# The eight-column time-step products spread over the projection unit that follows them

## Chip, cores and metric

The kernel runs on one core of one Trainium2 chip. The metric is the device time of one execution in microseconds (us); the kernel before has a median of 1232.65 us over 3 runs (1232.53 to 1235.9).

## The reference

Two transformer-like blocks follow each other on 256 tokens of width 1024, all in float32. The first block projects the normalised, modulated input `h` with one wide matrix and splits the result by columns; three mixers use the parts. The change concerns one part of eight columns, the raw time steps of the state-space mixer:

```python
h = rms_norm(x, g_pre_mix) * (1 + scale1) + shift1
(sc_b, sc_c, sc_x, q, k, v, z, xbc, dt_raw,
 gl_a, gl_b, gl_c) = split_columns(h @ w_in)
...
dt = jax.nn.softplus(dt_raw.astype(jnp.float32) + dt_bias.astype(jnp.float32))
a_neg = -jnp.exp(a_log.astype(jnp.float32))
y = ssd_scan(xh, dt, a_neg, bm, cm) + xh * d_skip.astype(jnp.float32)[:, None]
```

`dt_raw` is 256 tokens by 8 heads, a product over 1024 inputs. The second block ends in a feed-forward layer in which each token reads 128 experts from HBM.

## The kernel before, in words

Everything is written out by engine: each engine (PE for the matrix products, DVE, ACT and POOL for the rest, SP for most transfers) has its own program, and semaphores tie them together. Tokens are two tiles of 128 (`NT`), the width is eight chunks of 128 (`KC`). The weights come as units of 128 x 2048 float32 (1 MB) through a ring of three slots; the order of the units is the list `ORDER` (three "xbc", three "sc", two "qk", one "v", two "z", twelve "gl", and so on), and SP loads a slot again when `unit_done` says that PE is through with its former unit.

The projection units up to ("sc", 0) are plain float32 products of `hT` (the transposed input) with the unit. From ("sc", 1) on (`FRONT0`), `proj_T` (line 559) makes the first half of the sum over the width in plain float32 (line 568: eight products, of which each stands as two records in the trace), and the second half from two rounded parts (`mm3`, lines 527 to 529: three products each, eight times, one record each). The rounded parts of a unit are written by ACT (`front_hi`, line 1259) and POOL (`front_lo`, line 1592); PE waits for them between the two halves (`front_parts`). ACT copies each finished unit out of its PSUM bank (line 1246).

Between the units ("sc", 0) and ("sc", 1) stand the time-step products (lines 661 to 665): for each of the 2 token tiles and 8 chunks, a 128 x 128 piece of `hT` is the stationary operand and 8 columns of `w_dt` are the moving one, 16 products, or 32 records. They accumulate in the PSUM bank `BX`, after a wait for its former reader (`evac` at 3). The last increments `dt_mm`.

DVE waits for `dt_mm` (line 1890) behind its 24 convolution steps (lines 1876 and 1879), makes three short steps that end in `dt_lin`, then sums the modulation units 8 and 9 (lines 1798 and 1801), and then waits for ACT's exponential (line 1305), which ACT makes only after it has copied ("sc", 2) out and split the unit after next. SP's loads of the modulation units 10 and 11 (line 433) wait for DVE's sums of 8 and 9 and stand in SP's program behind the load of ring unit 7 and before that of ring unit 8, the "v" unit.

Further on, PE has another batch of narrow products (line 926: 16 products with one column, 32 records) ahead of the products that are made in a pause (line 831). Lines 748 and 749 alternate 256-column and 128-column products; lines 689, 708, 709, 690 and 711 mix products over 64 partitions with such over 128.

Of the kernel before, what the change touches and what calls it, by code (L numbers as in the profile page):

```python
# [25 lines left out]
P = 128  # L26
D = 1024
T = 256
NT = T // P
KC = D // P  # L30
# [88 lines left out]
def build(nc, stream, mod_w, small, x, band, final_g, experts, out):  # L119
    with ExitStack() as ctx:  # L120
        start = {}
# [5 lines left out]
        def sem(name):  # L127
            return ctx.enter_context(nc.semaphore(name))
# [6 lines left out]
        def cut(t, at, *dims):  # L135

            n = int(np.prod(dims))
            v = t[:, at:at + n]
            if len(dims) == 2:
                return v.rearrange("p (a b) -> p a b", a=dims[0])  # L140
            if len(dims) == 3:
                return v.rearrange("p (a b c) -> p a b c", a=dims[0], b=dims[1])
            return v
# [12 lines left out]
        hT = hT_flat[:, :].rearrange("p (k t) -> p k t", k=KC)  # L156
# [12 lines left out]
        ps = ctx.enter_context(nc.psum_tensor("ps", [P, 8, 512], F32))  # L169
        BM, BX = 2, 7  # L170
# [20 lines left out]
        def c_(name, a=0, b=None):  # L191
            lo, hi = SMALL[name]
            return sm[:, lo + a:(hi if b is None else lo + b)]
# [47 lines left out]
        def query_arrived(h):  # L241
# [7 lines left out]
        sc = cut(areaA, 3090, 6, T)  # L249
# [83 lines left out]
        dt_mm, dt_lin, dt_exp, dt_one, dt_log, a_exp, a_ready = (  # L333
            sem("dt_mm"), sem("dt_lin"), sem("dt_exp"), sem("dt_one"), sem("dt_log"), sem("a_exp"), sem("a_ready"))
# [136 lines left out]
        def _(pe):  # L471
            mm = nc.tensor.matmul

            def arrived(kind, j):
                u = AT[kind, j]
                if kind == "wq":
                    pe.wait_ge(*query_arrived(j))
                    return query_w[j]
                if (kind, j) == ("wo2", 2):
                    pe.wait_ge(wo2_in, 16)  # L480
                    return spare[:, :]
                pe.wait_ge(w_in[u % RING], 16 * (u // RING + 1))
                return slot[u % RING]
# [23 lines left out]
            def gemm_T(w, bank, rhs, new=None):  # L507

                for b in range(2):
                    for k in range(KC):  # L510
                        if new is not None and b == 0:
                            hT_chunk(new, k)
                        at = (b * KC + k) * P
                        last = mm(ps[:, bank, b * T:(b + 1) * T], w[:, at:at + P], rhs[:, k, :],  # L514
                                  start=(k == 0), stop=(k == KC - 1))
                return last
# [8 lines left out]
            def mm3(o, lhs, rhs, start, stop, **kw):  # L525

                mm(o, lhs[1], rhs[0], start=start, stop=False, **kw)  # L527
                mm(o, lhs[0], rhs[1], start=False, stop=False, **kw)  # L528
                return mm(o, lhs[0], rhs[0], start=False, stop=stop, **kw)  # L529
# [14 lines left out]
            def bank_free():  # L544

                n = evacs[0]
                evacs[0] += 1
                if n >= 2:
                    pe.wait_ge(evac, n - 1)
                return n % 2  # L550

            def front_parts(u):

                if u == FRONT0:
                    pe.wait_ge(hq_lo_ready, 1)
                pe.wait_ge(front_lo_ready, u - FRONT0 + 1)
                return front_hi[u % 2], front_lo[u % 2]

            def proj_T(kind, j):

                u, w, bank = AT[kind, j], arrived(kind, j), bank_free()
                if u < FRONT0:
                    gemm_T(w, bank, hT).then_inc(unit_done, 1)
                    return
                for b in range(2):
                    for k in range(4):
                        at = (b * KC + k) * P
                        mm(ps[:, bank, b * T:(b + 1) * T], w[:, at:at + P], hT[:, k, :], start=(b == 0 and k == 0),  # L568
                           stop=False, skip_group_check=True)
                both = front_parts(u)  # L570
                for b in range(2):
                    for k in range(4):
                        last = mm3(ps[:, bank, b * T:(b + 1) * T], [v[:, b, k * P:(k + 1) * P] for v in both],
                                   [v[:, k, :] for v in (hq_h, hq_l)], False, k == 3, skip_group_check=True)
                last.then_inc(unit_done, 1)

            def transposes(n):
# [79 lines left out]
            xbc_part(2, 2, 3, 4, 5, 6, 7)  # L657
            evacs[0] = 3
            proj_T("sc", 0)
            pe.wait_ge(evac, 3)  # L660
            for t in range(NT):
                for k in range(KC):
                    last = mm(ps[:, BX, 8 * t:8 * t + 8], hT[:, k, t * P:(t + 1) * P],
                              c_("w_dt", 8 * k, 8 * k + 8), start=(k == 0), stop=(k == KC - 1))
            last.then_inc(dt_mm, 1)
            for j in range(1, 3):
                proj_T("sc", j)
            for j in range(2):
                proj_T("qk", j)
            w = arrived("v", 0)  # L670
            bank = bank_free()
            for t in range(NT):
                for k in range(4):
                    mm(ps[:, bank, t * T:(t + 1) * T], hT[:, k, t * P:(t + 1) * P], w[:, k * T:(k + 1) * T],
                       start=(t == 0 and k == 0), stop=False, skip_group_check=True)
            both = front_parts(AT["v", 0])
            for t in range(NT):
                for k in range(4):
                    last = mm3(ps[:, bank, t * T:(t + 1) * T], [v[:, k, t * P:(t + 1) * P] for v in (hq_h, hq_l)],
                               [v[:, k // 2, (k % 2) * T:(k % 2 + 1) * T] for v in both], False, k == 3,  # L680
                               skip_group_check=True)
            last.then_inc(unit_done, 1)

            def sb_scores(h, part, stop):

                r = slice(64 * (h % 2), 64 * (h % 2) + 64)
                q, k = qk[r, h // 2, :], qk[r, 2 + h // 2, :]
                if part == 0:
                    return mm(ps[:, B3 + h, 0:T], k[:, 0:P], q[:, :], start=True, stop=stop)
                return mm(ps[:, B3 + h, T:T + P], k[:, P:T], q[:, P:T], start=True, stop=stop)  # L690

            pe.wait_ge(evac, 8)
            for h in range(4):
                sb_scores(h, 0, True)
                last = sb_scores(h, 1, True)
# [3 lines left out]
            for j in range(12):  # L699
# [3 lines left out]
                if j == 2:  # L703
                    pe.wait_ge(sb_lk, 1)
                    for h in range(4):
# [5 lines left out]
                        last = mm(ps[:, B3 + h, T:T + P], c_("suffix"), sbl[:, h, T:T + P], start=False, stop=True)  # L711
                    last.then_inc(sb_sum, 1)
                if j in (3, 4):

                    t = j - 3
# [3 lines left out]
                    for b in range(4):  # L719
                        last = nc.tensor.transpose(ps[:, BX, b * P:(b + 1) * P], xbc[:, b, t * P:(t + 1) * P],  # L720
                                                   c_("ident"))
# [9 lines left out]
                if j == 6:  # L731
# [3 lines left out]
                    for h in range(4):  # L735
# [3 lines left out]
                        last = mm(o[:, P:T], v1[:, 1, 64 * h:64 * h + 64], sba[:, h, T:T + P], start=False, stop=True,  # L739
                                  skip_group_check=True)  # L740
# [4 lines left out]
                    for h in range(8):  # L745
# [3 lines left out]
                        last = mm(o[:, P:T], a_rep[:, 8 + h, :], c_("tri"), start=False, stop=True,  # L749
                                  skip_group_check=True)  # L750
                    last.then_inc(acs_mm, 1)
                if j == 7:

                    pe.wait_ge(dec_arg, 16)
                    for g in range(2):
                        r = slice(64 * g, 64 * g + 64)
                        mm(ps[:, B3 + g, 0:T], xbc[r, 4, 0:P], xbc[r, 5, :], start=True, stop=True)
                        last = mm(ps[:, B3 + g, T:T + P], xbc[r, 4, P:T], xbc[r, 5, P:T], start=True, stop=True)
                    last.then_inc(bc_mm, 1)
                if j == 8:  # L760

                    pe.wait_ge(w_ready, 16)
                    for h in range(8):
                        r = slice(64 * (h % 2), 64 * (h % 2) + 64)
                        b = h // 2
                        o = ps[r, B3 + 2 + b // 2, (b % 2) * T:(b % 2) * T + T]
                        mm(o, x_tok[:, 0, 64 * h:64 * h + 64], decay[:, h, 0:T], start=True, stop=True)
                        last = mm(o[:, P:T], x_tok[:, 1, 64 * h:64 * h + 64], decay[:, h, T:T + P], start=False, stop=True,
                                  skip_group_check=True)
                    last.then_inc(y_mm, 1)  # L770
                if j == 9:
# [3 lines left out]
                    for g in range(2):  # L775
                        for b in range(2):
                            last = mm(ps[:, BX, g * T:(g + 1) * T], c_("ones"), ysq[:, 2 * g + b, :], start=(b == 0),
                                      stop=(b == 1))
# [3 lines left out]
            for j in range(4):  # L782
# [8 lines left out]
                for n, y in enumerate((ya, yb)):  # L791
                    for b in range(2):
                        for k in range(2):
                            mm(ps[:, banks[n], b * T:(b + 1) * T], w[:, at:at + P], y[:, k, :],
                               start=(k == 0), stop=(k == 1))
# [3 lines left out]
                for b in range(2):  # L799
                    for k in range(4):  # L800
                        at = (4 * b + k) * P
                        last = mm3(ps[:, banks[2], b * T:(b + 1) * T], [v[:, at:at + P] for v in both],
                                   [v[:, k, :] for v in (yc_h, yc_l)], k == 0, k == 3)
# [7 lines left out]
            for t in range(NT):  # L811
                for j in range(2, 4):
                    last = wo_tile(j, t)
# [109 lines left out]
            for b in range(2):  # L923
                for k in range(KC):
                    at = (b * KC + k) * P
                    last = mm(ps[:, BX, b:b + 1], w[:, at:at + P], modT[:, 72 + k:73 + k], start=(k == 0),
                              stop=(k == KC - 1))
# [81 lines left out]
            for g in range(4):  # L1009
                o = ps[:, g // 2, (g % 2) * T:(g % 2) * T + T]  # L1010
                mm(o, u2[:, 0, g * P:(g + 1) * P], band_sb[:, 0, g, :], start=True, stop=True)
                last = mm(o[:, P:T], u2[:, 1, g * P:(g + 1) * P], band_sb[:, 1, g, P:T], start=False, stop=True,
                          skip_group_check=True)
# [11 lines left out]
            for g in range(4):  # L1025
                last = mm(ps[:, g // 2, (g % 2) * T:(g % 2) * T + T], c_("pool_w", g * P, (g + 1) * P),
                          pooled[:, g, :], start=True, stop=True)
# [1567 lines left out]
```

## Time and profile before

| | |
|---|---|
| median of 3 runs | 1232.65 us (1232.53, 1232.65, 1235.9) |
| the profiled execution's own time | 1235.79 us |
| its span in the trace | 1234.1 us |
| mean granted TensorE clock | 0.971 |
| PE busy / DVE busy / ACT busy / POOL busy | 90% / 71% / 40% / 38% |
| mean read rate of the memory | 334 GB/s |

The span runs from the first to the last instruction of the trace; the execution's own time is 1.7 us longer. The profiled execution is 3.1 us slower than the median of the runs. The granted clock is given as a share of full speed: 1.00 is 2.4 GHz, 0.50 is 1.2 GHz.

### The profile page before, as it was taken

The numbers are of one execution on the slowest core, as the hardware profiler recorded it, in microseconds if no ns is written. First come the engines' busy times: TensorE is split into PE (matmuls) and PEld (weight loads), VectorE is DVE, ScalarE is ACT, GpSimd is POOL, SyncE is SP. The second block draws the span as 40 slices with busy tenths as digits, with TensorE's granted clock in tenths as the row PEclk, the third lists the DMA queues.
The fourth block names the chain that finished last, engine by engine and source line by source line (L and its number), as shares of the span: only waits on it lengthen the run. The fifth ranks groups of instructions, "written<-read, shape, count | busy, mean of one in ns | idle before, by whom it ended". The sixth has DMA issues, their size and how long they took to land.

```text
span 1234.1 us, 14550 instructions
## 1 busy us (share of the span) xinstructions
PE 1105.7 (90%) x4858; PEld 738.4 (60%) x4858; DVE 879.7 (71%) x1944; ACT 495.1 (40%) x1134; POOL 468.3 (38%) x360
## 2 busy tenths in 40 slices
PE   3999999999999999999899999987777878778776
PEld 3899899969999998875555655423323333223222
DVE  6586468987888888837787957758668586685555
ACT  2225153263333335534544344433434334325334
POOL 0133333023554452303355445743533535444420
PEclk9999999999999999999999999999998988989998
DMA  9656775664767773664999999999999999999995
GB/s 382 260 208 235 283 265 198 239 240 171 314 281 281 314 320 157 228 249 166 419 392 422 421 422 421 421 422 421 421 422 421 422 421 422 421 420 422 420 422 204
DMA packets 57803, 413.07 MB, mean 335 GB/s; under 512 B 6544, under 2 KB 6544, under 8 KB 8208
## 3 DMA queue, kind: packets, MB, share of 16 engines
q0 software_dynamic: 41328, 296.24, 58.3%
q1 hardware_dynamic: 16272, 115.83, 23.8%
q8 instruction: 30, 0.49, 0.2%
q10 hardware_dynamic: 144, 0.26, 0.1%
q14 instruction: 29, 0.24, 0.1%
HBM read 411.26 MB, written 1.05 MB: 334 GB/s over the span
## 4 chain that ended last, share of the span: by engine, by line
PE 59%; DMA 30%; DVE 6%; ACT 3%; issue 1%; POOL 1%; SPq 0%; ACTq 0%; DVEq 0%; POOLq 0%
PE ps L1111 14%; PE ps L527 8%; PE ps L529 7%; PE ps L528 7%; DMA areas_seam<-in_experts,idx 6%; DMA spare<-in_experts,idx 6%; PE ps L568 5%; PE ps L514 4%; DMA areaB<-in_experts,idx 4%; DMA gate_area<-in_experts,idx 3%; DMA mod_ring<-in_experts,idx 3%; DMA ring<-in_experts,idx 3%; DMA ring<-in_experts,part_buf 2%; PE ps L640 2%; DMA areaB<-in_mod_w 2%; PE ps L494 1%
## 5 line engine op out<-in xcount | busy, mean ns | idle before, releaser
L1515 ACT ACTIVATE act<-now 128x1 f32<-128x1 f32 x256 | 50.8, 198 | 264.4 <-DVE now L2389 261.7
L1111 PE MATMUL ps<-areaB,mod_sum 128*128 128x512 f32 x232 | 114.0, 623 | 25.4 <-ACT mod_sum L1523 25.4
L1801 DVE SCALAR_TENSOR_TENSOR mod_sum<-mod_ring,cols,mod_sum 128x256 f32<-128x256 f32 x280 | 118.9, 499 | 0.0
L1612 POOL TENSOR_TENSOR w_lo<-ring,w_hi 128x512 fp32r<-128x512 f32 x41 | 97.8, 2402 | 45.1 <-ACT w_hi L1253 44.9
L1669 POOL DMA_INDIRECT areaB<-in_experts,idx x58 | 68.3, 1178 | 118.6 <-PE ps L1111 58.5
L1111 PE MATMUL ps<-ring,mod_sum 128*128 128x512 f32 x192 | 95.7, 630 | 15.8 <-ACT mod_sum L1523 15.1
L1523 ACT ACTIVATE mod_sum<-small,act 128x128 f32<-128x128 f32 x256 | 102.8, 402 | 16.1 <-ACT act L1519 0.4
L1253 ACT ACTIVATE w_hi<-ring 128x2048 fp32r<-128x2048 f32 x41 | 78.5, 1914 | 53.3 <-DMA ring<-in_stream 43.2
L527 PE MATMUL ps<-hT_h,w_lo 128*128 128x256 f32 x352 | 98.4, 279 | 0.8 <-DVE hid_l L2069 0.8
L2389 DVE CUSTOM_DVE_ANT_0 areaB<-areaB,xn 128x1024 f32<-128x1024 f32 x58 | 70.8, 1225 | 38.7 <-DMA areaB<-in_experts,idx 38.6
L529 PE MATMUL ps<-hT_h,w_hi 128*128 128x256 f32 x352 | 98.2, 279 | 0.0
L528 PE MATMUL ps<-hT_l,w_hi 128*128 128x256 f32 x352 | 98.1, 279 | 0.0
L1812 DVE TENSOR_TENSOR w_lo<-ring,w_hi 128x1536 fp32r<-128x1536 f32 x41 | 89.1, 2196 | 11.4 <-ACT w_hi L1253 11.3
L1111 PEld LDWEIGHTS ps<-areaB,mod_sum 128*128 128x128 f32 x232 | 43.4, 195 | 89.6 <-ACT mod_sum L1523 45.3
L1592 POOL TENSOR_TENSOR front_lo<-ring,front_hi 128x1024 fp32r<-128x1024 f32 x19 | 57.8, 3044 | 88.7 <-ACT front_hi L1259 88.7
L1111 PE MATMUL ps<-gate_area,mod_sum 128*128 128x512 f32 x156 | 77.9, 623 | 13.5 <-ACT mod_sum L1523 13.4
L2389 DVE CUSTOM_DVE_ANT_0 ring<-ring,xn 128x1024 f32<-128x1024 f32 x48 | 58.3, 1224 | 31.8 <-DMA ring<-in_experts,idx 31.6
L1519 ACT ACTIVATE act<-act,gate_buf 128x1 f32<-128x1 f32 x256 | 75.4, 295 | 9.3
L1111 PEld LDWEIGHTS ps<-ring,mod_sum 128*128 128x128 f32 x192 | 36.7, 200 | 69.5 <-issue 37.0
L1669 POOL DMA_INDIRECT ring<-in_experts,idx x47 | 51.7, 1101 | 70.1 <-PE ps L1111 53.0
L2389 DVE CUSTOM_DVE_ANT_0 gate_area<-gate_area,xn 128x1024 f32<-128x1024 f32 x39 | 47.8, 1226 | 32.2 <-DMA gate_area<-in_experts,idx 32.1
L1111 PE MATMUL ps<-mod_ring,mod_sum 128*128 128x512 f32 x120 | 59.3, 618 | 9.3 <-ACT mod_sum L1523 8.8
(446 smaller groups left out, 2611.3 us busy)
## 6 DMA issues: line engine op xcount, KB each, us to landing
ring<-in_stream SPq DMA_DIRECT2D x75, 1024.0 KB, 6.0
mod_ring<-in_mod_w POOLq DMA_DIRECT2D x24, 1024.0 KB, 6.1
mod_ring<-in_mod_w SPq DMA_DIRECT2D x18, 1024.0 KB, 5.9
gate_area<-in_mod_w SPq DMA_DIRECT2D x3, 1024.0 KB, 13.2
areaB<-in_mod_w SPq DMA_DIRECT2D x3, 1024.0 KB, 22.9
gate_area<-in_stream SPq DMA_DIRECT2D x3, 1024.0 KB, 13.1
small<-in_small SPq DMA_DIRECT2D x1, 1352.0 KB, 28.7
x_sb<-in_x SPq DMA_DIRECT2D x1, 1024.0 KB, 9.0
```

Of the source, the lines that this page charges most:

```text
L527: mm(o, lhs[1], rhs[0], start=start, stop=False, **kw)
L528: mm(o, lhs[0], rhs[1], start=False, stop=False, **kw)
L529: return mm(o, lhs[0], rhs[0], start=False, stop=stop, **kw)
L1111: last = mm(ps[:, B3 + 2 * b + t, :], spread_w[n // FEW % 2][:, n % FEW, :], row[ROW_OF[n]][:, D + 512 * b:D + 512 * b + 512], start=first ...
L1253: A(w_hi[u % RING], slot[u % RING], ACT.Identity).then_inc(hi_ready, 1)
L1519: step(A(weight, weight, ACT.Identity, scale=gate_h[h % 2][:, t, n % TOPK:n % TOPK + 1]))
L1523: A(spread_w[n // FEW % 2][:, n % FEW, :], c_("ident"), ACT.Identity, scale=weight)\
L1612: nc.gpsimd.tensor_tensor(w_lo[s][:, HALF:], slot[s][:, HALF:], w_hi[s][:, HALF:].bitcast(F32), ALU.subtract).then_inc(lo_pool, 1)
L1669: pool.indirect_dma_start(row[ROW_OF[n]], None, experts, bass.IndirectOffsetOnAxis(ap=idx[:, n:n + 1], axis=0))\
L1801: ins = V.scalar_tensor_tensor(out=o[n], in0=w, scalar=vec[:, k:k + 1], in1=o[n], op0=ALU.mult, op1=ALU.add)
L1812: V.tensor_tensor(w_lo[s][:, 0:HALF], slot[s][:, 0:HALF], w_hi[s][:, 0:HALF].bitcast(F32), ALU.subtract).then_inc(lo_dve, 1)
L2389: V.tensor_tensor_reduce(u, u, xn[:, t, :], 1.0, 0.0, ALU.mult, ALU.add, now[n // FEW % 4][:, n % FEW:n % FEW + 1]).then_inc(dot_done, 1)
```

## The change

`proj_T` gets an argument, a function that it calls after each of the eight plain products (with 0 and the product's number) and after each of the eight threefold products (with 1 and the number). The time-step products of the first token tile are made in the first half of unit ("sc", 1), one after each of its plain products, those of the second tile in the second half. Only the very first of the sixteen now has `start` set. The wait for bank `BX` stays where it was; `dt_mm` is incremented by the last of them, which is PE's last product before unit ("sc", 2).

```diff
-            def proj_T(kind, j):
+            def proj_T(kind, j, between=None):
 
                 u, w, bank = AT[kind, j], arrived(kind, j), bank_free()
...
                         mm(ps[:, bank, b * T:(b + 1) * T], w[:, at:at + P], hT[:, k, :], start=(b == 0 and k == 0),
                            stop=False, skip_group_check=True)
+                        if between:
+                            between(0, 4 * b + k)
                 both = front_parts(u)
                 for b in range(2):
                     for k in range(4):
                         last = mm3(ps[:, bank, b * T:(b + 1) * T], [v[:, b, k * P:(k + 1) * P] for v in both],
                                    [v[:, k, :] for v in (hq_h, hq_l)], False, k == 3, skip_group_check=True)
+                        if between:
+                            between(1, 4 * b + k)
                 last.then_inc(unit_done, 1)
...
             proj_T("sc", 0)
             pe.wait_ge(evac, 3)
-            for t in range(NT):
-                for k in range(KC):
-                    last = mm(ps[:, BX, 8 * t:8 * t + 8], hT[:, k, t * P:(t + 1) * P],
-                              c_("w_dt", 8 * k, 8 * k + 8), start=(k == 0), stop=(k == KC - 1))
-            last.then_inc(dt_mm, 1)
-            for j in range(1, 3):
-                proj_T("sc", j)
+
+            def dt_product(t, k):
+
+                last = mm(ps[:, BX, 8 * t:8 * t + 8], hT[:, k, t * P:(t + 1) * P], c_("w_dt", 8 * k, 8 * k + 8),
+                          start=(t == 0 and k == 0), stop=(k == KC - 1), skip_group_check=True)
+                if t == NT - 1 and k == KC - 1:
+                    last.then_inc(dt_mm, 1)
+
+            proj_T("sc", 1, dt_product)
+            proj_T("sc", 2)
```

## Rows read from the trace of the kernel before

**Rows 1.** The page: span, granted clock in 40 slices, chain by engine.

```profile
span 1234.1 us, 14550 instructions
...
PEclk9999999999999999999999999999998988989998
...
PE 59%; DMA 30%; DVE 6%; ACT 3%; issue 1%; POOL 1%; SPq 0%; ACTq 0%; DVEq 0%; POOLq 0%
```

**Rows 2.** The chain that ended last, 50 to 80 us: start, us, what.

```profile
52.82 6.91 PE ps L514 x32
59.73 3.47 PE ps L663 x32
63.20 5.24 PE ps L568 x16
...
71.31 3.45 PE ps L568 x16
...
77.63 2.37 PE ps L568 x11
```

**Rows 3.** Single microseconds of the same stretch: busy times by engine, granted clock.

```profile
62.00:63.00 1.00, 1.00 (x11) 1.00 (x10) 1.00 (x1) 0.00 (x0) 1.00 (x1) 1.00 1.04 442
...
64.00:65.00 1.00, 1.00 (x4) 0.82 (x3) 1.00 (x3) 0.00 (x0) 0.07 (x1) 0.50 0.06 16
...
67.00:68.00 1.00, 1.00 (x6) 0.90 (x5) 0.97 (x6) 0.00 (x0) 0.00 (x0) 1.00 0.00 0
```

**Rows 4.** The chain, 460 to 640 us, and the clock of one microsecond in it.

```profile
473.16 3.46 PE ps L926 x32
476.63 3.52 PE ps L831 x8
...
481.02 0.86 PE ps L831 x4
...
478.00:479.00 1.00, 1.00 (x4) 0.82 (x3) 0.84 (x4) 1.00 (x4) 0.00 (x0) 0.50 0.00 0
```

**Rows 5.** Weight loads of the time-step products (name, count, shortest, median, longest in ns).

```profile
L663 PEld LDWEIGHTS ps<-small,hT x32: 190/192/192, 59.4 to 62.9; 128*128 128x128 f32 x32
```

**Rows 6.** Timeline of PE: wide and narrow float32 products in turn (lines 748, 749).

```profile
171.78 0.60 PE L748 MATMUL ps<-small,areaB 128*128 128x256 f32 x2
172.22 0.38 PE L749 MATMUL ps<-small,areaB 128*128 128x128 f32 x2
172.44 0.60 PE L748 MATMUL ps<-small,areaB 128*128 128x256 f32 x2
```

**Rows 7.** PE where 64 and 128 partitions alternate: one head, then the granted clock.

```profile
131.71 0.70 PE L689 MATMUL ps<-areaA 64*128 64x256 f32 x2
...
134.02 0.70 PE L689 MATMUL ps<-areaA 64*128 64x256 f32 x2
...
131.80:141.03 9.23, 9.23 (x41) 1.00 0.68 273
```

**Rows 8.** Timeline of DVE around the time steps.

```profile
54.02 13.62 DVE L1879 SCALAR_TENSOR_TENSOR areaA<-areaA,small 128x256 f32<-128x256 f32 x18
67.56 0.16 DVE L1891 TENSOR_TENSOR dtb<-ps,small 128x16 f32<-128x16 f32 x1
...
68.46 5.63 DVE L1801 SCALAR_TENSOR_TENSOR mod_sum<-mod_ring,cols,mod_sum 128x256 f32<-128x256 f32 x14
79.34 2.33 DVE L1900 TENSOR_SCALAR dtb<-dtb 128x16 f32<-128x16 f32 x1 [5.26 <-ACT dtb L1305]
```

**Rows 9.** Timeline of POOL: the rounded parts of units ("sc", 1) and ("sc", 2).

```profile
57.08 2.53 POOL L1592 TENSOR_TENSOR front_lo<-ring,front_hi 128x1024 fp32r<-128x1024 f32 x1
61.39 2.69 POOL L1592 TENSOR_TENSOR front_lo<-ring,front_hi 128x1024 fp32r<-128x1024 f32 x1 [1.78 <-ACT front_hi L1259]
```

**Rows 10.** SP's loads of modulation units 10, 11; ACT's split of ring unit 8.

```profile
73.72 0.80 SPq L433 DMA_DIRECT2D mod_ring<-in_mod_w  x2
...
85.32 1.06 ACT L1259 ACTIVATE front_hi<-ring 128x1024 fp32r<-128x1024 f32 x1 [0.74 <-DMA ring<-in_stream]
```

## The prediction

> **What bounds the kernel now.** The page comes first: the chain that ended last is PE for 59% of its length and transfers for 30%, and the clock row shows almost full speed in the stretch of the change [rows 1]. So a step that leaves PE shorter near the start should carry through, unless another engine or a transfer is close behind. The chain in order of time shows that here nothing but PE stands on it [rows 2]: unit ("sc", 0) from 52.82, the 32 time-step records from 59.73, the plain half of ("sc", 1) from 63.20, and so on without a gap. Two things are to be read there. The 32 records take 3.47 us, 108 ns each, although each moves only eight columns. And the plain half of ("sc", 1), 16 records, takes 5.24 us, where the same half of ("sc", 2) takes 3.45 us.
>
> The reason for the second is in the microseconds of that stretch [rows 3]: the clock is 1.00 (2.4 GHz) during the narrow records and 0.50 (1.2 GHz) after them, and back at 1.00 at 67. PE had been busy the whole time before it fell, with nothing but narrow products in its last 3.5 us. The price of the low clock is 5.24 - 3.45 = 1.79 us. The same picture comes once more: 32 one-column records from 473.16 to 476.63, then the clock at 0.50, and eight records of line 831 in 3.52 us, where four of them at the full clock take 0.86, so eight 1.72 [rows 4]. Price: 1.80 us. Both batches are followed by a fall in this execution; nothing shows that they are in every one.
>
> **The change, part by part.**
>
> *The 16 products themselves.* None is removed, none added. Their rate is set by the stationary load: each takes 192 ns as recorded [rows 5], and one starts every 108 ns. Placed after a wide product, a narrow one still needs its load, and the next wide one needs its own, which can only be hidden under the narrow one. The nearest row for that is the alternation of 256 and 128 columns [rows 6]: four records in 172.44 - 171.78 = 0.66 us; two wide ones at 3.45 / 16 = 0.216 us [rows 2] leave 0.23 for two narrow ones, so 0.11 each. A narrow record between wide ones costs what it costs in a batch. 32 x 0.108 = 3.47 before; 32 x 0.115 = 3.7 at most by this row. The lower bound is a narrow record that hides altogether: 0 instead of 3.47 us, which no row shows. I take the alternating row, as it is the nearest: a change of 0 to +0.2 us, and 0.1 in the sum.
>
> The Trainium skill ("TensorE: Matmul & The Clock Gate", in the section on why the gap is 56 ns and not 53.3 ns) says that the start-to-start distance of products never falls below some 25 ns however few columns there are, and its opening table says that weight loads are pulled ahead of products in flight. By these two, 32 well hidden records would cost an estimated 0.8 us. The 0.66 us of rows 6 speak against it.
>
> *The change of kind.* In the second half the narrow float32 products stand between products of rounded operands: 8 insertions, 16 changes of kind. Each unit now has two such changes. ("sc", 2) lasts from 71.31 to 77.63, 6.32 us [rows 2]: 3.45 for the plain half, 2.87 for 24 records, 0.120 each, and nothing left for a change. I take 0. The upper bound is from a stretch where products over 64 and over 128 partitions alternate: one head, ten records (four wide, six narrow), takes 134.02 - 131.71 = 2.31 us [rows 7], against 4 x 0.216 + 6 x 0.11 = 1.52, so 0.8 us for four changes, 0.2 each. Over 16 changes that is 3.2 us, over all 32 places 6.4. That row changes the partitions, which this change does not.
>
> *The clock.* After the change no stretch holds narrow products alone: in the first half two records of 0.216 us stand to two of 0.11, in the second three of 0.12 to two. The stretch of rows 7, over 9 us of wide and narrow mixed with gaps between, has 1.00 throughout. So the fall at 63 us should be gone: -1.79 us in an execution that had it, and 0 in one that had not.
>
> *The start of ("sc", 1).* It moves forward by 3.47 us, to 59.73. Its rounded part is written by 57.08 + 2.53 = 59.61 [rows 9], and it is asked for only after the plain half with its eight insertions, at about 59.73 + 3.45 + 1.8 = 65.0. That of ("sc", 2) is done at 64.1, needed after 73. No new wait for PE.
>
> *The later `dt_mm`.* It moves from 63.20 to 59.73 + 3.45 + 2.87 + 3.5 = 69.6. DVE is ready for it at 67.56 [rows 8], so it waits some 2 us where it waited for nothing. Behind that wait are the three short steps and the sums of units 8 and 9, which then end near 76.1 in place of 74.1. Next DVE waits for ACT's exponential, 5.26 us long now; that comes 1.8 us earlier if the clock does not fall, so about 1.5 us of wait are left. Price 0; if the cover were gone, 2 us of DVE, not of PE. ACT gets `dt_lin` at 70 and asks for it after 75.
>
> *SP's queue.* The loads of units 10 and 11 follow DVE's sum and go out at about 75.7 in place of 73.72 [rows 10], in front of the load of ring unit 8, due when ("sc", 2) is over, at 69.5 + 6.3 = 75.8. Three megabytes then land at about 85, when unit 8 landed before too (ACT waited 0.74 us for it, to 85.32). ACT's split ends at 86.4, POOL's part at 2.7 [rows 9] more is there at 89.1, and PE asks for it two units and a plain half after the start of ("qk", 0), 77.63 + 2 x 6.32 + 3.45 = 93.7 before, 91.9 now. It is nearly 3 us from being a wait. Price 0.
>
> **The sum** against the profiled execution: 1.79 - 0.1 = 1.7 us less, span 1232.4, own time 1234.1. Against the median another reading is needed. The profiled execution is 1235.79, one of the three runs is 1235.9, the other two are 1232.53 and 1232.65, and the distance of 3.1 to 3.4 us is near the sum of the two falls, 1.79 + 1.80 = 3.6. The likeliest reading is that the clock falls behind both batches in some executions and behind neither in others, and that the median is one of the others. Then there is nothing to win in it: 1232.65 + 0.1, rounded 1232.7.
>
> **The rivals.** A difference of 0.3% (3.7 us) is about what a measurement of this kernel can tell from no change.
>
> (A) The forecast, nothing in the median: 1232.7 us, chance 0.46.
>
> (B) The fall at 63 us is in the median execution too, and the 3.3 us between the runs have another cause. For it: the profiled execution has it. Then 1232.65 - 1.7 = 1230.9 us. If the shift also takes the batch at 473 us out of its fall, 1229.1. Chance 0.30, the last part of it 0.04.
>
> (C) The narrow products hide under the wide ones. Against it: rows 6. 1232.65 - 3.47 = 1229.2, and 1227.4 with the clock. Chance 0.05.
>
> (D) The other side: each change between narrow and wide costs as in rows 7, on PE, on the path. 16 x 0.2 = 3.2 gives 1235.9, 32 x 0.2 = 6.4 gives 1239.1 (1237.3 if a fall goes). It decides from 3.7 / 32 = 0.12 us for each place on. Against it: the 6.32 us of a unit with two changes. Chance 0.07.
>
> (E) The median execution of the new kernel is one in which the clock falls behind the second batch alone, while the old median had neither: 1232.7 + 1.8 = 1234.5. Chance 0.12.
>
> That the change does not do what it says is hardly open: the batch either stands in the trace as one piece or does not.
>
> **How the numbers follow.** 1232.7 is the time of (A). From 1229.8 to 1235.2 the range takes in (A), (B) without its last part, and (E), and leaves out (C), most of (D) and the double gain, 0.16 or so with some noise. Faster by over 0.3%, below 1228.95, needs (C) with the clock or more than (B) gives: 0.05. Slower, above 1236.35, needs (D) at its upper bound: 0.05. The same: 0.90.
>
> **What would show it.** In the new profile: line 568 of ("sc", 1) and the inserted records in turn from about 59.7, the unit over at 69.5 (9.8 us for both); granted clock 1.00 from 60 to 70; DVE idle for 2 us before its step at 67.56; its wait for ACT shorter; no wait of PE before ("sc", 1)'s second half or in "v". (C) would show as a unit well under 9 us, (D) as one of 13 us or more. The forecast is wrong if the runs of the new kernel are below 1231.5 with the clock low in the old one's runs, which makes it (B), or above 1235.

## The result, and the profile after

In 21 runs of each kernel the changed kernel takes 1237.73 us (1235.07 to 1241.54) and the kernel before 1235.9 us (1232.49 to 1238.99). The ratio is 1.0021, with a 95% interval of 1.0013 to 1.0028. The change costs 2.6 us by the ratio. That is within the 0.3% named as what a measurement can tell, but outside the forecast range of 1229.8 to 1235.2 us, and it is slower where no change was forecast. The kernel before, too, has a higher median than the three runs that were known: 14 of its 21 runs take 1235.1 us or more, 7 take 1233.8 or less, and two of the three were among the 7. The profiled execution has a span of 1237.0 us against 1234.1.

| us | before | after |
|---|---|---|
| unit ("sc", 0), line 514, starts | 52.82 | 53.12 |
| unit ("sc", 2), line 568, starts | 71.31 | 69.83 |
| SP loads modulation units 10, 11 | 73.72 | 78.13 |
| the "v" unit has landed (ACT's split starts) | 85.32 | 89.24 |
| 16 records of line 494 behind the first "gu" units | 294.44 | 297.46 |
| span | 1234.1 | 1237.0 |

The starts of PE in the table and in the sums are those of the chain. The timeline puts the start of a group some 0.15 us earlier (69.67 for the 69.83 here).

The timeline of PE in the changed kernel shows the unit with the inserted products [rows 2]:

```profile
60.44 0.68 PE L568 MATMUL ps<-hT,ring 128*128 128x256 f32 x2
60.95 0.28 PE L668 MATMUL ps<-small,hT 128*128 128x8 f32 x2
61.09 0.68 PE L568 MATMUL ps<-hT,ring 128*128 128x256 f32 x2
...
65.47 0.29 PE L668 MATMUL ps<-small,hT 128*128 128x8 f32 x2
...
66.05 0.28 PE L668 MATMUL ps<-small,hT 128*128 128x8 f32 x2
...
69.67 3.70 PE L568 MATMUL ps<-hT,ring 128*128 128x256 f32 x16
...
94.99 0.39 PE L527 MATMUL ps<-front_hi,hq_l 128*128 128x256 f32 x1 [2.01 <-POOL front_lo L1599]
```

A plain product with its insertion comes every 0.65 us, a threefold one with its insertion every 0.58 us, so the narrow pair costs 0.22 in both, and a change of kind costs nothing. PE is 1.5 us ahead at ("sc", 2), although it started 0.3 us later. The last line is new: PE waits 2 us for POOL in the "v" unit. Ahead of the same unit's plain half it already waits for the unit itself:

```profile
89.26 3.72 PE L681 MATMUL ps<-ring,hT 128*128 128x256 f32 x16 [0.38 <-DMA ring<-in_stream]
```

From the start of ("sc", 2) to the second half of "v" PE takes 25.3 us (69.67 to 94.99), where it took 22.2 before (71.15 to 93.38). Of these 3.1 us the two waits show 2.4. The rest does not appear as idle time, as the ends of the records ahead of a wait are modelled. What leads to both waits stands on the other engines. First DVE, then one of its steps by itself, then SP [rows 8, 10]:

```profile
69.85 0.17 DVE L1898 TENSOR_TENSOR dtb<-ps,small 128x16 f32<-128x16 f32 x1 [1.90 <-PE ps L668]
...
70.75 7.75 DVE L1808 SCALAR_TENSOR_TENSOR mod_sum<-mod_ring,cols,mod_sum 128x256 f32<-128x256 f32 x14
```

```profile
71.54 2.60 DVE L1808 SCALAR_TENSOR_TENSOR mod_sum<-mod_ring,cols,mod_sum 128x256 f32<-128x256 f32 x1
```

```profile
78.13 0.80 SPq L433 DMA_DIRECT2D mod_ring<-in_mod_w  x2
78.97 0.43 SPq L423 DMA_DIRECT2D ring<-in_stream  x1
```

The chain of work from 80 us on takes up the thread. In the kernel before nothing but PE stood on it here:

```profile
78.97 10.24 DMA ring<-in_stream
89.24 1.07 ACT front_hi L1266
90.38 4.58 POOL front_lo L1599
94.99 0.39 PE ps L527
```

DVE waits 1.90 us for the last narrow product. Its 14 steps of sums then take 7.75 us, where they took 5.63 in [rows 8]: one of them takes 2.60 us where the shortest takes 0.47, and it starts at 71.54, while POOL's split of a weight unit runs (71.35 to 73.85). SP's two modulation loads wait for these sums, and the load of the "v" unit stands behind them. It goes out at 78.97, 2.7 us after ("sc", 2) is over and it could have gone. Three megabytes asked for within 1.3 us take till 89.24 (a fourth is asked for at 82.59), and ACT, POOL and PE follow one by one.

The clock is at 1.00 where it had fallen to 0.50 [rows 3], and at 0.50 where it had been at 1.00. From the single microseconds of the changed kernel (the granted clock is the third number from the end of a line):

```profile
64.00:65.00 1.00, 1.00 (x8) 0.91 (x7) 1.00 (x3) 0.00 (x0) 0.38 (x1) 1.00 0.22 82
...
280.00:281.00 1.00, 1.00 (x6) 1.00 (x6) 0.90 (x3) 0.98 (x2) 1.00 (x3) 0.50 0.95 401
```

The table closes with this: 0.3 us from the start of the execution, -1.8 us to the start of ("sc", 2), +3.0 us up to the products behind "v" (line 689 starts at 96.59 before, and its successor, line 696, at 98.12), +1.5 us between 260 and 294 us. The sum is 3.0, and the spans differ by 2.9.

### The profile page after: what moved, and what is told of

It reads as the page before. It is cut to its first block, busy times and chain, and to the rows that moved or that the text cites. A ratio compares the mean times of both kernels' runs of the same rounds, so it can differ in the third digit from the quotient of the medians.

```text
span 1237.0 us, 14550 instructions
## 1 busy us (share of the span) xinstructions
PE 1101.6 (89%) x4858; PEld 736.3 (60%) x4858; DVE 877.0 (71%) x1944; ACT 495.3 (40%) x1134; POOL 468.5 (38%) x360
## 4 chain that ended last, share of the span: by engine, by line
PE 55%; DMA 30%; DVE 8%; ACT 4%; POOL 1%; issue 1%; SPq 0%; ACTq 0%; DVEq 0%; POOLq 0%
PE ps L1118 14%; PE ps L527 7%; PE ps L528 7%; PE ps L529 7%; DMA areas_seam<-in_experts,idx 6%; DMA spare<-in_experts,idx 6%; PE ps L514 4%; PE ps L568 4%; DMA areaB<-in_experts,idx 3%; DMA mod_ring<-in_experts,idx 3%; DMA gate_area<-in_experts,idx 3%; DMA ring<-in_experts,idx 3%; DMA ring<-in_experts,part_buf 2%; PE ps L644 2%; DMA areaB<-in_mod_w 2%; PE ps L494 1%
## 5 line engine op out<-in xcount | busy, mean ns | idle before, releaser
L1260 ACT ACTIVATE w_hi<-ring 128x2048 fp32r<-128x2048 f32 x41 | 78.5, 1914 | 53.1 <-DMA ring<-in_stream 43.1
L1819 DVE TENSOR_TENSOR w_lo<-ring,w_hi 128x1536 fp32r<-128x1536 f32 x41 | 89.1, 2196 | 11.4 <-ACT w_hi L1260 11.3
```

The source lines that it names most:

```text
L1260: A(w_hi[u % RING], slot[u % RING], ACT.Identity).then_inc(hi_ready, 1)
L1819: V.tensor_tensor(w_lo[s][:, 0:HALF], slot[s][:, 0:HALF], w_hi[s][:, 0:HALF].bitcast(F32), ALU.subtract).then_inc(lo_dve, 1)
```

## The experiments

My theory after the result had two parts: the loss is a wait handed on from DVE over SP's queue to PE, and what the spread products gain in clock is given back in a fall near 275 us (279 in the changed kernel). The rival was that the inserted products themselves cost PE more than the batch. All ratios are to the kernel before, run on the same chip.

**1. DVE's sums ahead of its wait** (changed kernel).

```diff
+            mod_units(8, 10)
             dve.wait_ge(dt_mm, 1)
...
             V.tensor_scalar(lin, lin, 0.0, None, ALU.max).then_inc(dt_lin, 1)
-            mod_units(8, 10)
```

> The changed kernel, with DVE's sums of modulation units 8 and 9 moved ahead of its wait for the time-step products. Theory Q (the loss is a wait handed on: DVE's later sums hold back SP's loads of units 10 and 11, these hold back the load of the v unit, and PE waits for its rounded part): the sums end near 74 us, SP issues the loads of 10 and 11 by 74.5, the load of the v unit goes out at 76.3, PE has no wait in the v unit, and the time is 2.4 us below the changed kernel's, level with the kernel before or up to 1.8 us under it (ratio 0.9985 to 1.000). Rival R (the inserted products cost PE more than the batch, wherever they make other work wait): the unit ends where it does now and the time stays 1.5 us or more above the kernel before (ratio 1.0012 or more).

Measured: 0.9999 (0.9986 to 1.0011). PE has no wait in "v"; SP issues the two loads at 70.83. (The times of this profile, and of most that follow, lie up to 3 us ahead of those of the changed kernel from the start on, for a reason that experiment 7 shows.) The stall is gone with the products still spread over both halves.

**2. SP's loads of 10 and 11 behind the "v" unit** (changed kernel).

```diff
-MODS_BEHIND_LOAD = {2: 8, AT["sc", 1] + RING: 10, AT["qk", 1] + RING: 12, AT["z", 1] + RING: 14,
+MODS_BEHIND_LOAD = {2: 8, AT["sc", 2] + RING: 10, AT["qk", 1] + RING: 12, AT["z", 1] + RING: 14,
```

> The changed kernel, with SP's loads of modulation units 10 and 11 put behind the load of the v unit in place of ahead of it. Theory Q: the v unit lands by 83 us, ACT splits it right after its copy of the first qk unit, PE has no wait in v, DVE still waits 1.9 us for the time steps and its sums still end near 78.5, and the time is about 2.4 us below the changed kernel's (ratio to the kernel before 0.9985 to 1.000). Rival R: as slow as the changed kernel, ratio 1.002. A third (the two loads come too late for DVE's next sums, and that is passed on): DVE waits for them at 86 us and the gain is 1 us or less.

Measured: 0.9997 (0.9987 to 1.0007), no wait of PE in "v". DVE waits as long for PE (1.89 us) and its sums take as long (7.75) as in the changed kernel; the whole profile lies 2.7 us earlier. This makes it the cleanest of the four: the late sums do no harm once the load of the weights does not queue behind them.

```profile
67.16 0.17 DVE L1898 TENSOR_TENSOR dtb<-ps,small 128x16 f32<-128x16 f32 x1 [1.89 <-PE ps L668]
...
68.06 7.75 DVE L1808 SCALAR_TENSOR_TENSOR mod_sum<-mod_ring,cols,mod_sum 128x256 f32<-128x256 f32 x14
```

**3. All sixteen in the first half** (changed kernel).

```diff
                         if between:
                             between(0, 4 * b + k)
+                            between(1, 4 * b + k)
...
-                        if between:
-                            between(1, 4 * b + k)
```

> The changed kernel, with all sixteen products in the first half of the unit, two after each plain product, none in the second half. The last of them is then over at 60.0 + 3.45 + 3.6 = 67.1 us, before DVE asks for them at 67.9. Theory Q: DVE does not wait, the sums end at 74 to 75, no wait of PE in v, ratio 0.9985 to 1.000. Rival R: ratio 1.002. The clock stays at 1.00 between 60 and 70 us by my reading, since two wide records stand to four narrow ones; if it falls there, 1.8 us come back.

Measured: 0.9995 (0.9985 to 1.0005). DVE does not wait, the sums take 5.63 us, PE does not wait, the clock stays at 1.00 in this unit.

**4. The late wait alone** (kernel before, batch in place).

```diff
             dve.wait_ge(dt_mm, 1)
+            dve.wait_ge(unit_done, DONE("sc", 1))
```

> The kernel before, its products in one batch as they were, but DVE waits for the end of unit (sc, 1) before it reads the time steps. Theory Q: this alone brings the loss: DVE waits 2 us (3.7 where the clock has fallen behind the batch), the v unit lands 3 to 5 us later, PE waits 2 to 4 us in v, and the time is 2 to 3 us above the kernel before (ratio 1.0015 to 1.0025). Rival R: nothing happens, ratio 1.000, as no product was spread.

Measured: 1.0040 (1.0026 to 1.0055). From the list of waits, 50 to 110 us:

```profile
DVE dtb L1892 <- PE ps L529: 3.8, 1, 3.8
...
PE ps L527 <- POOL front_lo L1592: 2.0, 1, 2.0
```

The same chain without a single product moved, so the rival is out. It is worse than the changed kernel and worse than expected. The batch and the fall behind it are as in the kernel before, so nothing is gained ahead of the wait, which is 3.77 us for DVE; and in its profile the clock falls at 98 and at 282 us as well. PE lies 3.4 us behind the first profile of the kernel before at the second half of "v" (96.80 against 93.38), 4.9 us at the first product of line 873 (278.82 against 273.94), and 6.4 us at the records of line 494 (300.68 against 294.27): the two further falls come with 1.5 us each.

**5. The batch, with the sums first** (kernel before; the edit of experiment 1).

> The kernel before with its batch, only DVE's sums of units 8 and 9 moved ahead of its wait for the time steps, as in the first experiment. Against that experiment it tells the spread apart from the batch with the wait out of the way. If the fall of the clock behind the batch were in every execution, this one would be 1.7 us slower than the spread products with the same DVE order (ratio to the kernel before 1.000 against 0.9986). If the fall only comes in some executions, or comes back in another place, the two are level within 0.6 us.

Measured: 1.0000 (0.9988 to 1.0013), level with the spread products in the same order. The two intervals reach 1.5 us either way, so the times alone do not rule out the 1.7 us named in the expectation; the profile is clearer. The fall behind the batch is there in it (0.50 at 63 us), and the one near 275 is not.

**6. First half and loads behind, together.**

> The candidate: all sixteen products in the first half of the unit, and SP's loads of units 10 and 11 behind the load of the v unit. Both repairs cure the same wait, so together they should give no more than one: ratio 0.999 to 1.000, PE without a wait in v. If it is below 0.9985, something else than the wait and the clock is in play.

Measured: 1.0003 (0.9990 to 1.0016), no wait of PE in "v". The second repair adds nothing that the runs show.

**7. The kernel before once more**, one execution with its profile.

> The kernel before, unchanged, for a second profile. Two readings of the first profile are open: the clock falls behind the batch at 63 us in every execution, or only in some. If the first granted rise of the clock comes some 2 us earlier here than at 36.3 us, as it did in the profiles of the first three experiments, the time is near 1232.6 and I expect no fall behind the batch; if it comes at 36, I expect the fall and 1235.8.

Measured: 1232.84 us, span 1231.1. The time came as expected, the missing fall did not: the clock rises early, at 30.1 us, and falls behind the batch all the same.

```profile
30.00:31.00 1.00, 0.79 (x5) 0.38 (x3) 1.00 (x3) 0.00 (x0) 0.00 (x0) 0.95 0.91 385
...
61.00:62.00 1.00, 1.00 (x4) 0.81 (x3) 1.00 (x2) 0.00 (x0) 0.54 (x1) 0.50 0.34 131
```

The chain in order of time has the same 3.47 and 5.24 us as [rows 2], 2.5 us sooner:

```profile
50.29 6.91 PE ps L514 x32
57.19 3.47 PE ps L663 x32
60.66 5.24 PE ps L568 x16
```

In the first profile the clock rose at 36.3 us. Thus 2.5 of the 3 us between these two executions are there at 57 us, from when the clock rises first and not from whether it falls later. That all executions of the two groups differ by this is likely, but only these two of this kernel have a profile.

**8. The batch made twice** (kernel before).

```diff
-            for t in range(NT):
+            for t in [0, 1, 0, 1]:
```

> The kernel before with the sixteen products made twice in a row (the second time over the first). The batch takes 6.94 us in place of 3.47. If only the products cost, the time rises by 3.47 us (ratio 1.0028). If a fall of the clock is now made certain where it was not before, it rises by 3.47 + 1.8 = 5.3 us against the executions without a fall (ratio 1.0035 to 1.0043), and the profile shows 0.50 within the batch or behind it. DVE should not wait, or for under 0.2 us (the batch ends at 66.7).

Measured: 1.0050 (1.0035 to 1.0065), some 6 us. The clock is at 0.50 from 64.3 to 74.5 us. The 64 narrow records take 9.61 us in the chain, not 6.94: once the clock has fallen within them, they are slower too, an estimated 0.21 us each in place of 0.108 (38 of them fit before 64.3, which leaves 26 for the last 5.5 us). DVE, which was not to wait, waits 1.73 us.

**9. PE's later work put back in its old place** (experiment 3 and four products that nothing reads).

```diff
             proj_T("sc", 1, dt_product)
+            for _ in range(4):
+                mm(ps[:, BM, T:2 * T], c_("ident"), hT[:, 0, :], start=True, stop=True)
             proj_T("sc", 2)
```

> The kernel with all sixteen products in the first half of the unit, and behind that unit four more wide products whose result nothing reads (eight records, 1.72 us). They put the rest of PE's work back to where it lies in the kernel before. What is asked: in the spread kernels so far the clock fell at 273 to 279 us, in the stretch where PE waits for the second normalised input, and in the batch kernels without a late wait it did not. If that depends on where in time the stretch lies, the fall at 273 to 279 is gone here and none at 63 takes its place: the four products cost 1.72 and give 1.4 back, ratio 1.0000 to 1.0008 to the kernel before. If the stretch now falls in any case, the time is 1.7 us above the first-half kernel (ratio 1.001 to 1.0015) and the profile shows 0.50 near 275.

Measured: 1.0004 (0.9992 to 1.0017). PE does 1.72 us more work than in experiment 3 and the time is the same within the intervals. The profile has no fall at 63 and none near 275, which is the first of the two outcomes set out above; the ratios alone (0.9995 and 1.0004, chips apart) would not tell the two apart.

**10. The two pauses filled** (experiment 3 and four products that nothing reads, at lines 873 and 881 of the kernel before).

```diff
+                def fill():
+                    for _ in range(2 if new == 1 else 0):
+                        mm(ps[:, BM, T:2 * T], c_("ident"), c_("keys", 0, T), start=True, stop=True)
...
                 def step(j, n):
...
+                    if (j, n) in ((0, 0), (0, 1)):
+                        fill()
                     if n:
```

> The kernel with all sixteen products in the first half, and four wide products whose result nothing reads in PE's two pauses of 0.95 and 0.83 us ahead of the products of line 873 and 881 (two in each, 0.86 us), so at no cost if they fit. If the fall at 273 to 279 comes from the little work in that stretch, it goes, and the time is 1.4 us below the first-half kernel: ratio 0.9985 to 0.9992 to the kernel before, the first version under it. If the fall stays, the ratio is 0.9995 to 1.0003, as it was.

Measured: 0.9988 (0.9977 to 0.9998). The stretch near 275 is now at the full clock. The same microsecond, first in experiment 3:

```profile
274.00:275.00 1.00, 1.00 (x7) 1.00 (x6) 1.00 (x3) 1.00 (x1) 1.00 (x2) 0.50 0.58 229
```

and here:

```profile
274.00:275.00 1.00, 1.00 (x11) 1.00 (x10) 1.00 (x3) 1.00 (x1) 1.00 (x3) 1.00 0.75 279
```

In this profile, however, the gain does not last. At the first one-column record PE is 1.4 us ahead of experiment 3 (469.27 against 470.70); the clock then falls within that batch, at 471.8, and stays low till 478.7, where it was low from 474.4 to 477.8 in experiment 3; and at 479 PE is 0.2 us behind (the next records of line 831 of the kernel before start at 478.93 against 478.72). So the better ratio rests on the eleven times, not on the profile.

**11. The same four products in the kernel before**, as a control.

> The control for the last one: the kernel before with its batch, and the same four wide products in the pauses. There was no fall in that stretch to take away, so the ratio should be 1.0000, or up to 1.0003 if the products do not quite fit; the fall behind the batch at 61 to 64 us stays.

Measured: 0.9998 (0.9987 to 1.0008), the fall behind the batch still there. By the time the filler costs nothing that shows, and it is of no use while the batch stands.

**12. The second batch mixed as well** (experiment 10 and the one-column products of line 926 with wide ones between them).

```diff
                     last = mm(ps[:, BX, b:b + 1], w[:, at:at + P], modT[:, 72 + k:73 + k], start=(k == 0),
-                              stop=(k == KC - 1))
+                              stop=(k == KC - 1), skip_group_check=True)
+                    if k % 4 == 2:
+                        products_in_pause(1)
             last.then_inc(shift_mm, 1)
-            products_in_pause(4)
```

> The last version (products in the first half, four wide products in the two pauses near 271 us), and at the second batch of narrow products, the one-column ones at 473 us, the four wide products of the pause that follows are made between them, one after every fourth, in place of behind them. No product is added. If a stretch of nothing but narrow products is what the clock falls behind, the fall at 472 to 479 us goes too, and up to 0.8 us more is saved, no more because DVE's normalised tile, not PE, is what the transposes then wait for: ratio 0.9980 to 0.9988 to the kernel before. If it stays, the ratio is that of the last version, 0.9988.

Measured: 0.9987 (0.9974 to 0.9999), about 1.6 us under the kernel before. The falls behind both batches [rows 2 to 4] and the one near 275 are gone. From the timeline of PE:

```profile
476.39 0.68 PE L837 MATMUL ps<-small 128*128 128x256 f32 x2
476.90 0.28 PE L938 MATMUL ps<-modT,mod_ring 128*128 128x1 f32 x2
478.42 1.09 PE L829 MATMUL ps<-small,xn 128*128 128x128 f32 x8 [1.24 <-DVE xn L1765]
```

As expected, PE then waits (1.24 us) for DVE. The ratios of experiments 10 and 12 do not tell the two apart. Its profile has a span of 1231.8 us; the first one of the kernel before, in which the clock also first rises late (36.3 us there, 37.0 here), has 1234.1. Experiments 10 and 12 are the versions that beat both kernels. Their intervals reach 0.9998 and 0.9999, so the gain is small and just clear of none, and they are the best two of eleven ratios.

## Why the prediction was wrong

*The products themselves*: right. "0 to +0.2 us" for their cost, from the alternating row, against 0.22 us a pair in both halves. *The change of kind*: right at 0; rival (D) is out by experiments 1 to 3. Rival (C) is out for loads of this kind, and with it the estimate of 0.8 us that the prediction worked out from the Trainium skill ("TensorE: Matmul & The Clock Gate"): the pair costs the same 0.22 us in any company. The 25 ns of that page are a lower limit, and 0.11 us for a record does not speak against it.

*The later `dt_mm`*: the wait of 2 us came out as 1.90. But the step took the sums behind it at the 5.63 us of [rows 8] and set their end at 76.1; they took 7.75 and ended at 78.5. POOL's split now runs wholly inside them. In experiment 3, where they start earlier, they take 5.63 again and POOL's split 5.07 in place of 2.50. One of the two is longer by some 2 us when they meet; what decides which was not tried. The trace of the kernel before had such a meeting already, twenty microseconds on, in two rows that the prediction did not look at:

```profile
90.11 7.73 DVE L1801 SCALAR_TENSOR_TENSOR mod_sum<-mod_ring,cols,mod_sum 128x256 f32<-128x256 f32 x14
```

```profile
91.93 2.46 POOL L1592 TENSOR_TENSOR front_lo<-ring,front_hi 128x1024 fp32r<-128x1024 f32 x1 [2.82 <-ACT front_hi L1259]
```

*SP's queue*: this is the step that failed. The queue was named, and the two loads and the "v" unit behind them, but the loads were set at 75.7 and the landing at 85, "when unit 8 landed before too". They went out at 78.13, and the landing was at 89.24. The three megabytes took 11.1 us from the first issue, so even from 75.7 they would have come at an estimated 86.8; the prediction gives no row for its 85. POOL's part was taken at 2.7 us and took 4.58, again beside DVE's sums. It was there at 94.96 and not at 89.1, and PE's second half of "v", which would have followed at 92.0 (the 3.27 us of the plain half before, from 88.7), started at 94.99. So the "nearly 3 us" of cover were in truth a delay of 3.0 us, shown as waits of 0.38 and 2.01. Experiment 4 has the wait without the spread, experiments 1 to 3 the spread without the wait.

*The clock*: the price of the fall behind the batch, 1.79 us, was right (5.24 us for the plain half again in experiment 7), and so was that the mixed stretch has none: of the eight spread versions profiled, with the changed kernel, none shows a fall there. The reading that the median execution has no fall (A) was wrong. Six of six profiled executions with the batch show it, rival (B)'s condition. The execution of 1232.84 us in experiment 7 has both falls, which takes away the ground of (E) as well. The first rise comes at 30.1 to 31.5 us in eight of the fourteen profiles and at 36.3 to 37.0 in six; in the two of the kernel before it accounts for 2.5 of the 3 us. Yet (B) did not come either, as the gain is given back. The execution of experiment 3 is 1.16 us ahead of that of experiment 7 at the first product of line 873 (270.33 against 271.49; it had begun the unit ("sc", 0) 0.42 us later), and 0.19 us behind it at the records of line 494 (292.18 against 291.99). No profile of a plain batch kernel without the late wait has a fall between 270 and 283, and every profile of a spread one without filler or move has it. Experiments 9 and 10 remove it, one by moving the stretch, one by filling it, with one profile each.

*The base*: 1232.7 us was the median of three runs carried over, and two of the three happened to lie in the faster group: over 21 runs the same kernel has 1235.9. So 3.2 of the 5.0 us between forecast and measured time come from the base, and a kernel equal to the one before would have lain above the range too. The change itself costs 1.8 us by the medians, 2.6 by the ratio. In the profiles this is what the delay of 3.0 us behind the queue leaves, with 1.8 us gained in the clock ahead of it and 1.5 lost in the clock behind it.

## What to carry to other kernels

A step that is moved later is to be followed over the other engines' queues to the transfers behind them, with the durations of work that will now coincide, not those of the row where it ran alone. A cover of 3 us that is the sum of four estimated steps is no cover; it should have stood in the forecast as a range. A base of three runs is thin where runs come in two groups 3 us apart. And a low clock that is cured in one place can come back in the next stretch with pauses, so a gain in clock is only counted at the end of the chain.

## What the runs showed of the hardware

Three things had not been expected. PE busy with narrow products alone, without any idle time, is followed by the clock of 1.2 GHz, in all six batch profiles here (with the batch made twice it falls within it) and at the one-column batch near 473 us in all fourteen profiles but that of experiment 12 (in experiment 10 it falls within that batch). The Trainium skill ("TensorE: Matmul & The Clock Gate", in its part on oscillation) describes the fall for idle gaps between bursts; the traces show it behind a stretch in which PE was busy throughout, and gone when the same products stand between wide ones.

And whether a stretch with short pauses, as the one near 275 us, is followed by a fall seems to depend on when it comes. Against the profile of the kernel before with the same kind of first rise, the first product of line 873 comes 1.2 to 1.6 us earlier in experiments 1, 2, 3 and 6, 1.6 us later in the changed kernel and 4.9 us later in experiment 4, and the clock falls in all six; it comes 0.1 to 0.4 us later in experiments 5, 9 and 11 (the last with its filler) and 7.4 us later in experiment 8, and it does not fall. What sets the two kinds apart was not tried. Why the first rise comes at one of two times, some 6 us apart, which makes 2.5 us of the 3 us between the two executions of the kernel before, stays open too.

The third is how DVE's sums and POOL's split meet. Either one of DVE's steps takes 2.60 us in place of 0.47 and the split its usual 2.50 (changed kernel), or the sums take their usual 5.63 and the split ends 2.2 us after them, however early it began: 76.33 after 74.09 in the kernel before, 74.24 after 71.99 in experiment 3, 94.96 after 92.75 in the changed kernel's "v" unit.
